# The sink attention's queries and keys in a two-layer hybrid kernel: turned in two steps, and scans put elsewhere among the maxima

## The reference, cut to what matters

```python
SSM_WIDTH, ATTN_WIDTH, N_Q_HEADS, N_KV_HEADS, HEAD_DIM, ROPE_DIM = 512, 512, 8, 2, 64, 16
...
        u = proj[..., :SSM_WIDTH]
        q = proj[..., SSM_WIDTH:SSM_WIDTH + ATTN_WIDTH]
        k = proj[..., SSM_WIDTH + ATTN_WIDTH:SSM_WIDTH + ATTN_WIDTH + KV_WIDTH]
        v = proj[..., SSM_WIDTH + ATTN_WIDTH + KV_WIDTH:]
        y_ssm = s5_mixer(u, ...)
        q = partial_rotary(q.reshape(bsz, L, N_Q_HEADS, HEAD_DIM), positions)
        k = partial_rotary(k.reshape(bsz, L, N_KV_HEADS, HEAD_DIM), positions)
        y_attn = sliding_window_sink_attention(q, k, v, attn_sinks[l])
        merged = jnp.concatenate([rms_norm_2(y_ssm, ...), rms_norm_2(y_attn, ...)], axis=-1)
...
def partial_rotary(t, positions):          # the first 16 of 64 channels of each head
    rot = jnp.concatenate([t1 * cos - t2 * sin, t2 * cos + t1 * sin, tf[..., ROPE_DIM:]], axis=-1)
...
    # attention, for each block of 128 queries and each head
    s = jnp.einsum('bqhgd,bkhd->bhgqk', q_blk, k_blk).astype(jnp.float32) * scale
    s = jnp.where(valid, s, MASK_VALUE)
    m = jnp.maximum(jnp.max(s, axis=-1, keepdims=True), sink)
    p = jnp.exp(s - m)
    p = p / (jnp.sum(p, axis=-1, keepdims=True) + jnp.exp(sink - m))
    return jnp.einsum('bhgqk,bkhd->bqhgd', p.astype(v_blk.dtype), v_blk)
...
    # s5_mixer: a complex linear recurrence over time
    _, _, xr, xi = lax.associative_scan(_s5_combine, (a_re, a_im, bu_re, bu_im), axis=1)
```

## Time and profile before

| | us |
|---|---|
| median of 3 runs | 798.84 (797.82 to 799.75) |
| the profiled execution's own time | 795.62 |
| its span in the profile | 793.8 |
| mean granted TensorE clock | 0.996 |

### The profile page before, as it was taken

How to read it: one execution, slowest core, us unless ns; L and a number is a source line. 1 busy time by engine, 2 the same in 40 slices (tenths; PEclk the granted TensorE clock), 3 DMA queues, 4 the chain that set the end, 5 groups by cost and what they waited for, 6 DMA issues and landing times.

```text
span 793.8 us, 12695 instructions
## 1 busy us (share of the span) xinstructions
PE 776.1 (98%) x5133; PEld 679.3 (86%) x5133; DVE 513.3 (65%) x753; ACT 405.3 (51%) x649; POOL 232.8 (29%) x186
## 2 busy tenths in 40 slices
PE   7999999999999999999999999998999999999996
PEld 6889988999888889987778888987887888888885
DVE  4756864764547657865557965766678776777453
ACT  5754436534565545344335545717766555556341
POOL 3031895570742000036009910126002111011010
PEclk9999999999999999999999999999999999999999
DMA  8997895387721554654545556430363656655651
GB/s 218 213 266 217 208 207 150 82 193 170 167 81 51 187 173 147 213 171 147 158 136 158 179 195 185 135 132 2 119 220 127 199 186 210 187 176 172 220 177 54
DMA packets 77821, 130.72 MB, mean 165 GB/s; under 512 B 4414, under 2 KB 28210, under 8 KB 77634
## 3 DMA queue, kind: packets, MB, share of 16 engines
q1 hardware_dynamic: 76418, 125.00, 54.4%
q0 software_dynamic: 1200, 4.83, 1.9%
q10 hardware_dynamic: 144, 0.07, 0.0%
HBM read 128.82 MB, written 1.06 MB: 164 GB/s over the span
## 4 chain that ended last, share of the span: by engine, by line
PE 94%; DVE 2%; ACT 2%; issue 1%; DMA 1%; POOL 0%; DVEq 0%; SPq 0%; POOLq 0%; ACTq 0%
PE ps L1508 15%; PE ps L1516 15%; PE ps L1512 15%; PE ps L1548 10%; PE ps L1527 6%; PE ps L1531 6%; PE ps L1535 6%; PE ps L1552 5%; PE ps L1615 2%; PE ps L1634 2%; PE ps L1647 1%; PE ps L1646 1%; PE ps L1645 1%; PE ps L1925 1%; PE ps L1790 1%
## 5 line engine op out<-in xcount | busy, mean ns | idle before, releaser
L914 DVE TENSOR_TENSOR w_lo<-stage,w_hi 128x1024 fp32r<-128x1024 f32 x226 | 296.1, 1329 | 164.8 <-ACT w_hi L627 164.4
L627 ACT ACTIVATE w_hi<-stage 128x1024 fp32r<-128x1024 f32 x232 | 242.5, 1061 | 237.1 <-PE ps L1516 116.8
L1508 PE MATMUL ps<-w_hi,act_t 128*128 128x512 f32 (+1 forms) x376 | 102.5, 396 | 3.1 <-issue 2.6
L1516 PE MATMUL ps<-w_lo,act_t 128*128 128x512 f32 (+1 forms) x376 | 99.6, 388 | 1.0 <-issue 1.0
L1548 PE MATMUL ps<-act_t,w_hi 128*128 128x512 f32 x352 | 88.3, 393 | 0.7 <-DVE act_t L951 0.7
L1508 PEld LDWEIGHTS ps<-w_hi,act_t 128*128 128x128 f32 x376 | 68.4, 189 | 18.5 <-issue 5.7
L1516 PEld LDWEIGHTS ps<-w_lo,act_t 128*128 128x128 f32 x376 | 70.2, 190 | 15.7 <-issue 1.2
L1512 PE MATMUL ps<-w_hi,act_t 128*128 128x512 f32 (+1 forms) x312 | 82.3, 387 | 0.0
L1548 PEld LDWEIGHTS ps<-act_t,w_hi 128*128 128x128 f32 x352 | 63.3, 189 | 12.1 <-issue 0.9
L1512 PEld LDWEIGHTS ps<-w_hi,act_t 128*128 128x128 f32 x312 | 58.0, 189 | 12.0
L1527 PE MATMUL ps<-act_t,w_hi 128*128 128x256 f32 x416 | 58.8, 284 | 0.0
(11 more groups left out here) (364 smaller groups left out, 1195.4 us busy)
## 6 DMA issues: line engine op xcount, KB each, us to landing
stage<-in_even_w_in SPq DMA_DIRECT2D x64, 512.0 KB, 5.7
stage<-in_odd_w_in SPq DMA_DIRECT2D x48, 512.0 KB, 4.2
stage<-in_w_gate_up SPq DMA_DIRECT2D x44, 512.0 KB, 4.6
stage<-in_w_down SPq DMA_DIRECT2D x22, 512.0 KB, 4.5
stage<-in_even_w_out SPq DMA_DIRECT2D x16, 512.0 KB, 4.3
stage<-in_odd_w_out SPq DMA_DIRECT2D x16, 512.0 KB, 4.1
stage<-in_w_in SPq DMA_DIRECT2D x10, 512.0 KB, 3.7
stage<-in_w_out SPq DMA_DIRECT2D x8, 512.0 KB, 4.9
```

The source lines that it names most:

```text
L627: nc.scalar.activation(w_hi[:, u % RING, :], stage[:, u % RING, :], ACT.Copy).then_inc(hi_ready, 1)
L914: nc.vector.tensor_tensor(w_lo[:, u % RING, :], stage[:, u % RING, :], w_hi[:, u % RING, :].bitcast(F32), ALU.subtract).then_inc(lo_ready, 1)
L1508: mm(out[:, b, :], a_hi(k)[:, tok[b]], hi[:, i, :], start=(k == 0), stop=False)
L1516: ins = mm(out[:, b, :], a_hi(k)[:, tok[b]], lo[:, i, :], start=False, stop=(k == k_tiles - 1))
```

## The change

The rotation is split in two: `rope` takes the heads that it rotates as arguments, and VectorE runs it once for the eight query heads, right behind the last `ssm_drive` and without waiting for keys, and once for the keys (each key head stands twice, so four of them). ScalarE copies both halves of the keys ahead of both halves of the values, and signals `k_out` between them. TensorE turns all eight query tiles ahead of `ssm_lags(0)`, and the four key tiles between `ssm_lags(0)` and `ssm_lags(1)`; ScalarE then copies the turned queries first and the keys last. VectorE's scan 2 moves from behind head 33's maximum to ahead of the keys' rotation, and scan 3 from behind head 34's maximum to behind head 33's.

```diff
--- before.py
+++ after.py
@@ -276,7 +276,7 @@
         drive_done, drive_read, v_ready, scan_done, state_ready, y_done = (sem(n) for n in ("drive_done", "drive_read", "v_ready", "scan_done", "state_ready", "y_done"))
         b_pow_ready, c_pow_ready, lag_done, lag_copied, lag_ready, fade_ready = (sem(n) for n in ("b_pow_ready", "c_pow_ready", "lag_done", "lag_copied", "lag_ready", "fade_ready"))
         gelu_hi_ready, gelu_ready, gelu_lo_ready = sem("gelu_hi_ready"), sem("gelu_ready"), sem("gelu_lo_ready")
-        rope_ready, qk_turned, qk_ready = sem("rope_ready"), sem("qk_turned"), sem("qk_ready")
+        rope_q_ready, rope_k_ready, k_out, qk_turned, qk_ready = (sem(n) for n in ("rope_q_ready", "rope_k_ready", "k_out", "qk_turned", "qk_ready"))
         ret_stats = sem("ret_stats")
         sink_sum, sink_exped, y_attn_ready = sem("sink_sum"), sem("sink_exped"), sem("y_attn_ready")
         sig_ready, ssm_out_ready = sem("sig_ready"), sem("ssm_out_ready")
@@ -811,19 +811,21 @@
                                            scale=rstd_in_q[:, b:b + 1])
             ins.then_inc(drain_sem(("sq", 0)), 1)
             chunk_done(act, ("skv", 0))
+            kv = [result(("skv", 0), 256)[:, b, :].rearrange("p (h d) -> p h d", d=HD) for b in range(NB)]
             for b in range(NB):
-                heads = result(("skv", 0), 256)[:, b, :].rearrange("p (h d) -> p h d", d=HD)
-                nc.scalar.activation(qkv[:, b, K_AT:V_AT, :].rearrange("p (k r) d -> p k r d", r=2), heads[:, 0:KV_H, :].unsqueeze(2).to_broadcast([P, KV_H, 2, HD]),
-                                     ACT.Copy, scale=rstd_in[:, b:b + 1])
-                ins = nc.scalar.activation(qkv[:, b, V_AT:V_AT + KV_H, :], heads[:, KV_H:2 * KV_H, :], ACT.Copy, scale=rstd_in[:, b:b + 1])
+                ins = nc.scalar.activation(qkv[:, b, K_AT:V_AT, :].rearrange("p (k r) d -> p k r d", r=2), kv[b][:, 0:KV_H, :].unsqueeze(2).to_broadcast([P, KV_H, 2, HD]),
+                                           ACT.Copy, scale=rstd_in[:, b:b + 1])
+            ins.then_inc(k_out, 1)
+            for b in range(NB):
+                ins = nc.scalar.activation(qkv[:, b, V_AT:V_AT + KV_H, :], kv[b][:, KV_H:2 * KV_H, :], ACT.Copy, scale=rstd_in[:, b:b + 1])
             ins.then_inc(drain_sem(("skv", 0)), 1)
 
             act.wait_ge(qk_turned, 1)
             nc.scalar.activation(q_t[:, 0:2, :].rearrange("p m n -> p (m n)"), bank(2), ACT.Copy)
             act.wait_ge(qk_turned, 2)
-            nc.scalar.activation(k_t[:], bank(1).rearrange("p (k n) -> p k n", k=2), ACT.Copy).then_inc(qk_ready, 1)
+            nc.scalar.activation(q_t[:, 2:4, :].rearrange("p m n -> p (m n)"), bank(3), ACT.Copy)
             act.wait_ge(qk_turned, 3)
-            nc.scalar.activation(q_t[:, 2:4, :].rearrange("p m n -> p (m n)"), bank(3), ACT.Copy).then_inc(qk_ready, 1)
+            nc.scalar.activation(k_t[:].rearrange("p m n -> p (m n)"), bank(1), ACT.Copy).then_inc(qk_ready, 1)
             for n in range(32, 41):
                 if n in (33, 35, 37):
                     split_hi(next_unit[0] + 1)
@@ -1268,18 +1270,19 @@
                     ins = nc.vector.tensor_tensor_scan(flat(ssm_b[:, ct, c]), flat(fade[:, w, :]), flat(ssm_a[:, ct, c]), 0.0, ALU.mult, ALU.add)
                 ins.then_inc(scan_done, 1)
 
-            def rope():
-
-                lo8, hi8 = qkv[:, :, 0:V_AT, 0:ROPE_HALF], qkv[:, :, 0:V_AT, ROPE_HALF:2 * ROPE_HALF]
-                shape = [P, NB, V_AT, ROPE_HALF]
-                tmp = [rope_tmp[:, i * 192:(i + 1) * 192].rearrange("p (b h d) -> p b h d", b=NB, d=ROPE_HALF) for i in range(4)]
+            def rope(first, heads, at, turned_heads):
+
+                view = qkv[:, :, first:first + heads, :]
+                lo8, hi8 = view[:, :, :, 0:ROPE_HALF], view[:, :, :, ROPE_HALF:2 * ROPE_HALF]
+                shape, size = [P, NB, heads, ROPE_HALF], NB * heads * ROPE_HALF
+                tmp = [rope_tmp[:, at + i * size:at + (i + 1) * size].rearrange("p (b h d) -> p b h d", b=NB, d=ROPE_HALF) for i in range(4)]
                 cosb, sinb = (sm[n][:, ST:NA].rearrange("p (b d) -> p b d", b=NB).unsqueeze(2).to_broadcast(shape) for n in ("cos", "sin"))
                 TT(tmp[0], lo8, cosb, ALU.mult)
                 TT(tmp[1], hi8, sinb, ALU.mult)
                 TT(tmp[2], hi8, cosb, ALU.mult)
                 then(TT(tmp[3], lo8, sinb, ALU.mult))
                 TT(lo8, tmp[0], tmp[1], ALU.subtract)
-                TT(hi8, tmp[2], tmp[3], ALU.add).then_inc(rope_ready, 1)
+                TT(hi8, tmp[2], tmp[3], ALU.add).then_inc(turned_heads, 1)
 
             take_row(2)
             chunk_done(dve, ("u", 0))
@@ -1300,14 +1303,16 @@
             ssm_drive(2)
             ssm_drive(3)
             chunk_drained(dve, ("sq", 0))
-            chunk_drained(dve, ("skv", 0))
-            rope()
+            rope(0, SINK_H, 0, rope_q_ready)
             ssm_scan(1)
+            ssm_scan(2)
+            dve.wait_ge(k_out, 1)
+            rope(K_AT, V_AT - K_AT, NB * SINK_H * ROPE_HALF * 4, rope_k_ready)
             for i in range(8 + 3):
                 if i < 8:
                     score_max(32 + i, 2)
-                if i in (1, 2):
-                    ssm_scan(i + 1)
+                if i == 1:
+                    ssm_scan(3)
                 if i >= 8:
                     split_lo(next_unit[0] + 1)
                 if i == 8:
@@ -1820,30 +1825,26 @@
             for j in range(2):
                 tokens_unit(("skv", 0), j, x_hi, x_lo, KD)
 
+            heads_of = lambda b, first: qkv[:, b, first:first + 2, :].rearrange("p h d -> p (h d)")
+            pe.wait_ge(rope_q_ready, 1)
+            for m in range(4):
+                for b in range(NB):
+                    ins = nc.tensor.transpose(ps[:, 2 * BANK + m * S + b * P:2 * BANK + m * S + (b + 1) * P], heads_of(b, 2 * m), ident[:])
+                if m % 2 == 1:
+                    ins.then_inc(qk_turned, 1)
             ssm_lags(0)
-            ssm_lags(1)
-            pe.wait_ge(rope_ready, 1)
-            heads_of = lambda b, first: qkv[:, b, first:first + 2, :].rearrange("p h d -> p (h d)")
-            q_pair = lambda m, b: nc.tensor.transpose(ps[:, 2 * BANK + m * S + b * P:2 * BANK + m * S + (b + 1) * P], heads_of(b, 2 * m), ident[:])
-            for m in range(2):
-                for b in range(NB):
-                    ins = q_pair(m, b)
-            ins.then_inc(qk_turned, 1)
+            pe.wait_ge(rope_k_ready, 1)
+            chunk_drained(pe, ("skv", 0))
             for m in range(KV_H):
                 for b in range(NB):
                     ins = nc.tensor.transpose(bank(1, P, m * S + b * P), heads_of(b, K_AT + 2 * m), ident[:])
             ins.then_inc(qk_turned, 1)
-            for m in range(2, 4):
-                for b in range(NB):
-                    ins = q_pair(m, b)
-            ins.then_inc(qk_turned, 1)
+            ssm_lags(1)
             pe.wait_ge(qk_ready, 1)
 
             def ssm_between(i, part):
                 if part == 1 and i < 0:
                     ssm_lags(i + 4)
-                if part == 1 and i == 0:
-                    pe.wait_ge(qk_ready, 2)
                 if part == 1 and i in (1, 3, 5):
                     ssm_states(i // 2)
```

## The result

| | before | changed |
|---|---|---|
| median, first comparison (19 runs of each) | 797.1 us | 801.81 us |
| profiled execution: its own time, span | 795.62, 793.8 | 799.43, 797.6 |
| mean granted TensorE clock | 0.996 | 0.993 |

The ratio is 1.006, 95% interval 1.0046 to 1.0074: the change makes the kernel slower by 0.6%, 4.7 us. Measured twice more, it gave 1.0044 (1.0025 to 1.0064) and 1.0074 (1.0054 to 1.0094). The prediction said slower, 802.0 us.

A forecast was written before the change was run, and what follows sets the result against it. TensorE, carrying 94% of the chain that ended last, was taken to bound the kernel. The terms 3.6 - 0.1 - 1.25 + 1.0 gave +3.2 us, added to the median 798.84 for 802.0 us, range 796.4 to 803.6.

The forecast's parts named there:

- The sign: Whole kernel: slower, with chance 0.64, against 0.17 for the same and 0.19 for faster.
- the mechanism: VectorE instructions with both inputs in SBUF take turns with GpSimd instructions reading SBUF, which delays the keys' rotation.
- Rotation end, +3.6: On VectorE, the rotation that TensorE waits for ends at 543.25 instead of 539.67: +3.6 us.
- The sequence of turns: Keys' six instructions: two between L584 and L585, then one each after L585, L586, L583, L584, ending at 543.25.
- whatever their lengths: VectorE and GpSimd instructions reading SBUF were said to alternate one each, regardless of how long each is.
- TensorE's wait, 5.0: TensorE's wait ahead of the keys' turns grows from 1.02 to about 5.0 us.
- Behind it, -0.1: TensorE from rotated keys to first scores: 1.75 us with 0.05 of semaphore instead of 1.88, so -0.1 us.
- Scan 3, -1.25: With scan 3 between heads 33 and 34, TensorE's 1.26 us wait at head 35 goes: -1.25 us.
- Clock, +1.0: TensorE's clock falls after the long wait, for 2.8 us at the lower level: +1.0 us, range 0 to 1.7.
- few turns are lost: Rival: the keys' small rotations start at once and TensorE hardly waits; -2.75 us, 796.1 us, chance 0.19.
- Half the turns: Rival: three or four key instructions slip between L584 and L585; +0.1 to +1.0, 798.9 to 799.9 us, chance 0.16.
- Scan 3 gives nothing: Rival: at head 35 the 1.25 us is not won, so slower still; 803.2 us, chance 0.05.

The follow-up runs named there:

- e1: The changed kernel with GpSimd's four products of scan 1 held until the keys are rotated; ratio to the kernel before 0.9995 (0.9973 to 1.0016).
- e7: The changed kernel with the keys' rotation in twelve instructions of 32 columns instead of six of 64; one run, 803.85 us.
- e2: The changed kernel with 26 small unused products on TensorE between the first lags and the wait for rotated keys; ratio to the kernel before 1.0057.
- e4: The kernel before with scan 3 behind head 35's maximum instead of behind head 34's; ratio to the kernel before 0.9999 (0.9979 to 1.0018).
- e3: The changed kernel with the three scans where the kernel before has them; ratio to the kernel before 0.9993 (0.9975 to 1.0012).
- e5: The changed kernel with scan 1 behind the keys' rotation, scan 2 behind head 33, scan 3 behind head 35; ratio to the kernel before 0.9964, median 795.12 us.
- e6: The changed kernel with scan 2 behind the keys' rotation, scan 1 still ahead; ratio to the kernel before 1.0008 (0.9992 to 1.0024).

## Why the prediction was right, and where its numbers were off

The sign held, and so did the mechanism for the instructions of this kernel. The stage grew by 5.44 us, and TensorE's timeline splits it without a remainder: it comes to its wait 0.32 us sooner behind the keys' drain (1.99 instead of 2.31), waits 4.91 longer, needs 1.45 more from the keys' turns to the first scores and 0.73 more from there to `ssm_lags(2)`, and 1.33 less from there to `y_attn`.

* **Rotation end, +3.6.** From the last drive's end (532.84) to the keys' rotation's end (542.60) took 9.76 us; before it took 6.44, so +3.3. The sequence of turns came as written: the first after L584, the second in the gap, then one each after L585, L586, L583, L584. e1 shows the cause. One sentence of the working goes too far, that turns alternate "whatever their lengths": instructions of 32 columns go two to a turn (e7). For the 64 columns here it makes no difference.
* **TensorE's wait, 5.0.** It was 5.93. The working placed TensorE by before's profile, where it stood without work for about 1 us at 523.2, ahead of the stage; the profiles of the changed kernel lack that gap. So TensorE came to its wait some 1.3 us earlier against VectorE. That makes the stage longer and the part ahead of it shorter, which the sum against the total doesn't see.
* **Behind it, -0.1.** 1.74 us from the keys' turns to the first scores at full clock (e2) against 1.83 before: -0.1.
* **Scan 3, -1.25.** Held: 1.27 us at 548.99, no wait at heads 35 and 36, and 1.33 us less on TensorE from `ssm_lags(2)` on. e4 wins the same by another place.
* **Clock, +1.0: the step that was mis-sized.** I took the length of the low stretch from the earlier trace rows, 2.8 us. That cut it short even for the kernel before: in its 15:18 stretch 0.10 is still missing, another 0.6 us at the lower level, 3.4 in all. Here it lasted 6.8, of which 4.9 lay behind the wait. From the keys' turns to `ssm_lags(2)` TensorE took 4.87 us; 1.74 + 0.85 at full clock is 2.59 (e2). That is +2.3, more than the upper end I had given it (1.7). The stretch of before that the earlier trace rows leaves out:

```profile
15.00:18.00 3.00, 3.00 (x13) 2.48 (x12) 1.86 (x3) 3.00 (x7) 0.60 (x2) 0.90 1.07 168
```

The terms as measured give 3.3 - 0.1 - 1.3 + 2.3 = +4.2 us, where the sum had +3.2; with the 1.3 us of TensorE's earlier arrival it is the stage's 5.4. In the totals the kernel lost 4.7, 3.5 and 5.1 us in the three comparisons. The forecast of 802.0 came so close to 801.81 because it was added to 798.84, the median of three runs, while before's median over 19 was 797.1: an error of one and a half us in the sum was covered by one of the same size in its base. That closeness is luck.

Of the rivals, "few turns are lost" fell: all but one of the six waited. Its price, -2.75 us, was too high even for a kernel where it is true: with GpSimd held (e1) the stage is 2.1 us under before, and the total at most 2.2 (0.9973). "Half the turns" fell with the second instruction, which found the gap, and the third, which didn't. "Scan 3 gives nothing" fell.

What I didn't ask was which half of the change carries the loss. It is the two scans' place ahead of the keys: by the stage the split alone saves 1.4 us (e3), with a later scan 3 it saves 2.8 (e5, which the totals confirm), and with one scan left ahead of the keys it already loses 1.8 (e6). The idle 4.6 us on VectorE looked like room for scans; what it held was GpSimd's silence, and a scan ends that.

## What to carry to other kernels

* Before filling idle time of VectorE, look at what the filler releases on GpSimd. Here two scans that take 2.4 us alone (e1) started over 8 us of GpSimd work, and five of the six VectorE instructions on the path behind them then waited for a GpSimd instruction. Put such a release behind the short instructions that TensorE waits for.
* Short instructions on the path suffer most: six that need 1.0 us took 5.1. The maxima, with an input in PSUM, kept their 0.48 us beside GpSimd's products (551.03 of the changed kernel beside L583), so a rotation that read PSUM might pay no turns; that wasn't tried.
* Count a TensorE wait with the slower work that may follow it (1.6 us behind the 2.95 of e6, 2.3 behind the 5.93 here), not by its own length alone; and size a term by the stage it lies in, since a total of this kernel wanders by more than one such term.

## What the runs showed of the hardware that I had not expected

* A wait of 2.95 us in steady work was followed by a fall of the clock (e6), as the 1.02 us of before was not: 3.4 us at the lower level, and from the keys' turns to `ssm_lags(2)` 4.2 us (543.91 to 548.12) instead of 2.6. After 5.93 us it was 6.8 us, after 6.88 (e7) 6.8 as well.
* The length of a short wait does not settle whether the clock falls. Near 58 us of e5 a wait of 1.75 us in steady work was followed by 3.4 us at the lower level (0.92, 0.50 and 0.73 granted in 58:64). Near 11 us a wait of 2.63 us in before was followed by a fall (0.54 in 12:15), and one of 2.64 us at the same place of e4 was not. So e6's 2.95 us is one profile, and whether the clock always falls behind it is open.
* An instruction of 32 columns can be held as long as one of 64, but two or three of them go through between two GpSimd instructions, where one or two of 64 columns do (e7).
* The wait near 58 us differs from execution to execution by up to 4.0 us with the same program (none, none and 3.97 us in the changed kernel). Why the weights come late there in some stays open.
